# Weights of a second token stream fetched into two places of 1 MB instead of four places of 512 KB

## The reference

```
x = first_block(x, c, ctx, ...)                 # two layers, each with moe_ffn over 32 experts
return second_block(x, c_2, ctx_2, ...)

# second_block, layer 0
a_lat = x_lat * (1 + sc1) + sh1
a_ctx = x_ctx * (1 + csc1) + csh1
m_lat, m_ctx = mixer(a_lat, a_ctx, lp, rope, n_rows, not last)     # the same weights for both
x_ctx = layer_norm_2(DEEPNORM_ALPHA * x_ctx + (1 + cg1) * m_ctx, ln1_g[l], ln1_b[l])
f_ctx = swiglu(x_ctx * (1 + csc2) + csh2, w_ffn_gate[l], w_ffn_up[l], w_ffn_down[l])
```

## Time and profile before

| | |
|---|---|
| median of three runs | 3012.84 us |
| profiled execution: its time / its span | 3007.24 us / 3005.4 us |
| PE busy | 2720.4 us, 91% |
| DVE, ACT, POOL busy | 789.2, 456.2, 74.8 us |
| granted TensorE clock, mean | 0.958 |
| moved by the DMA engines | 764.86 MB, 254 GB/s over the span |
| of it the main stream's queue q1 | 680.57 MB |
| of it POOL's queue q0 | 74.26 MB |

### The profile page before, as it was taken

One profiled execution on the slowest core, in us unless ns is written; L12 is line 12 of the kernel. 1 busy time (PEld: TensorE's weight loads), 2 busy tenths in 40 slices (PEclk: granted clock), 3 DMA queues, 4 the chain that ended last, 5 costly groups with the idle time before them and its releaser, 6 DMA issues.

```text
span 3005.4 us, 33995 instructions
## 1 busy us (share of the span) xinstructions
PE 2720.4 (91%) x13754; PEld 1855.5 (62%) x13754; DVE 789.2 (26%) x1893; ACT 456.2 (15%) x973; POOL 74.8 (2%) x144
## 2 busy tenths in 40 slices
PE   6998988889989969988999779998999899998998
PEld 3554544445567754555555555687788646687887
DVE  1344202222121252111111333613642214413002
ACT  2132102121120021000000113401000123301000
POOL 0000000000000000000000000000000000000000
PEclk9998998989999979999999889999999999999999
DMA  9884898999977518999999622143675221233330
GB/s 402 332 337 186 364 414 342 372 415 411 422 305 273 224 71 330 412 418 422 416 422 422 275 83 102 70 155 114 250 278 225 113 84 56 85 142 137 141 140 15
DMA packets 117628, 764.86 MB, mean 254 GB/s; under 512 B 12832, under 2 KB 15648, under 8 KB 34272
## 3 DMA queue, kind: packets, MB, share of 16 engines
q1 hardware_dynamic: 94400, 680.57, 56.1%
q0 software_dynamic: 20224, 74.26, 6.4%
q10 hardware_dynamic: 2848, 7.83, 0.7%
HBM read 759.20 MB, written 3.41 MB: 254 GB/s over the span
## 4 chain that ended last, share of the span: by engine, by line
PE 76%; DMA 14%; DVE 6%; issue 2%; ACT 1%; SPq 1%; POOL 0%; ACTq 0%; DVEq 0%
PE bank L552 73%; DMA ring<-in_stream 13%; PE bank L851 1%; PE bank L840 1%; SPq L431 1%; DMA work<-in_stream 1%; PE bank L556 1%; DVE MX L1913 0%; DVE work L1851 0%; ACT work L1446 0%; DVE work L1930 0%; DVE work L1710 0%; DVE work L1703 0%; DVE X L2130 0%; ACT work L1376 0%
## 5 line engine op out<-in xcount | busy, mean ns | idle before, releaser
L552 PE MATMUL bank<-A,ring 128*128 128x256 f32 (+1 forms) x3088 | 712.4, 390 | 14.8 <-issue 7.7
L552 PEld LDWEIGHTS bank<-A,ring 128*128 128x128 f32 x3088 | 590.1, 192 | 131.4 <-issue 44.2
L552 PE MATMUL bank<-ring,A 128*32 128x512 f32 (+3 forms) x2304 | 413.2, 635 | 84.0 <-DMA ring<-in_stream 73.4
L552 PE MATMUL bank<-work,ring 128*128 128x256 f32 x1696 | 384.0, 383 | 5.7 <-DVE work L2382 2.1
L552 PEld LDWEIGHTS bank<-work,ring 128*128 128x128 f32 x1696 | 322.3, 191 | 57.0 <-issue 3.9
L552 PE MATMUL bank<-work 128*64 128x128 f32 (+5 forms) x2084 | 339.5, 333 | 14.8 <-DVE work L1788 5.2
L552 PEld LDWEIGHTS bank<-ring,A 128*32 128x32 f32 (+2 forms) x2304 | 129.6, 129 | 350.4 <-issue 221.0
L552 PE MATMUL bank<-A,work 128*128 128x256 f32 x1280 | 293.4, 386 | 20.0 <-ACT A L1344 11.4
L552 PEld LDWEIGHTS bank<-work 128*128 128x128 f32 (+2 forms) x2084 | 248.1, 172 | 79.1 <-issue 44.3
L552 PEld LDWEIGHTS bank<-A,work 128*128 128x128 f32 x1280 | 242.8, 193 | 79.7 <-issue 33.6
L552 PE MATMUL bank<-work,par_sb 128*128 128x256 f32 (+2 forms) x228 | 81.9, 498 | 66.2 <-DVE work L1703 15.5
(11 more groups left out here) (268 smaller groups left out, 1524.7 us busy)
## 6 DMA issues: line engine op xcount, KB each, us to landing
ring<-in_stream SPq DMA_DIRECT2D x648, 1024.0 KB, 12.7
work<-in_stream POOLq DMA_DIRECT2D x134, 512.0 KB, 8.8
X<-in_xt ACTq DMA_DIRECT2D x1, 2048.0 KB, 13.8
spill<-work ACTq DMA_DIRECT2D x3, 512.0 KB, 9.7
work<-spill POOLq DMA_DIRECT2D x3, 512.0 KB, 5.3
tab_sb<-in_tab_a ACTq DMA_DIRECT2D x1, 1120.0 KB, 18.5
X<-in_ctx2t ACTq DMA_DIRECT2D x1, 1024.0 KB, 15.9
out<-X SPq DMA_DIRECT2D x4, 256.0 KB, 2.3
```

Of the source, the lines that this page charges most:

```text
L552: return pay(pe.matmul(o, w, x, start=start, stop=stop, tile_position=place), tells)
```

## The change

```diff
-QTILES, QRING = 8, 4
+QTILES, QRING = 16, 2
```

## The result

The changed kernel takes 3034.27 us (median of 11 runs, 3023.42 to 3047.18), the kernel before 3006.83 us in 11 runs on the same chip. The ratio is 1.0079, with a 95% interval of 1.0059 to 1.0099: slower by 0.6 to 1.0%. One run of the experiments, of the kernel "rest", took 5618.34 us instead of some 3010 and is left out of its ratio.

What follows compares the result with a forecast made beforehand. PE was taken to bound the kernel, except where it waits for weights. Unhidden stall and clock loss of 18.3 us less 3.4 at the start gave 14.9, taken as +15 us: 3028 us, range 3009 to 3045 us.

Steps and rivals of the forecast that it cites:

- Landing: Context pieces beside ring traffic: a 1 MB piece lands 10.0 us after issue, against 8.8 us for 512 KB.
- The turns by rows: Context and ring queues alternate one partition row each, 4 KB against 8 KB before, so 1 MB lands 1.2 us later.
- Stalls: PE's waits for late context pieces: 5 x 4.0 + 3.6 + 3.2 + 0.8 = 27.6 us more.
- The six places with 10.0 us of room: Six context pieces with 10.0 us from possible issue to need: they come just in time, without a stall.
- The start: First context stage: the second 1 MB piece lands sooner than the old fourth piece, gaining 3.4 us.
- 7 x 1.7 = 11.9 us: Behind each of seven stalls PE's clock is halved for 3.4 us, costing 1.7 us each.
- What hides: Ring waits absorb part of the 39.5 us gross loss at the seven stalls, leaving 18.3 us.
- 5.7, against 6.5: 0: Stall at 1597 us: its 5.7 us loss hides fully in 6.5 us of ring waits, leaving 0.
- Rival 1: Expert stretches with full DMA engines: reserve suffices or stalls hide fully; +5 us, 3018 us; chance 0.22.
- Rival 2: Context transfers: larger rows are cheaper and the reserve suffices; -7 us, 3006 us; chance 0.08.
- Rival 3: Pieces land later, six more places stall, nothing hides: +50, perhaps a third hidden, +33, 3046 us; 0.20 together with rival 4.
- Rival 4: Transfers cut into 4 KB rows again, landing in 12.5 us: about +40, 3053 us; 0.20 together with rival 3.

Runs made afterwards that it cites:

- rest: Kernel before, with 57 of the 67 pieces at 1 MB, all but ten tight places, which keep two pieces of 512 KB; 3014.19 us, 1.0007.
- Split: Changed kernel's places and release, but each piece fetched as two 512 KB transfers, PE waiting for both; 3064.62 us, 1.0172 against the kernel before.
- filled: Changed kernel plus seven dummy matmuls ahead of each of the seven late pieces; 3013.38 us, 1.0006 against the kernel before.
- filler: Kernel before, 512 KB pieces, plus seven dummy matmuls at each of the seven places late at 1 MB; 3014.69 us, 1.0019.
- seven: Kernel before, with 1 MB pieces at the seven late places only; 3033.0 us, 1.0067.
- late: Changed kernel's release by 16 tiles, but two 512 KB transfers with a wait each; 3014.4 us, 1.0006 against the kernel before.
- small: Kernel before, with context pieces of 4 tiles (256 KB) in eight places; 3006.39 us, 0.9986.
- start: Kernel before, with only its first 32 context tiles as two 1 MB transfers; 3003.71 us, 0.9976, and on another chip 3006.19 us, 0.9999.
- combo: Kernel before, with first 32 context tiles as two 1 MB transfers and all later ones as 256 KB pieces; 3001.19 us, 0.9979.
- The third profile: The changed kernel unaltered, profiled a third time on the chip of the last experiments; one run, 3028.18 us.
- The two timed comparisons: The changed kernel against the kernel before, first 3034.27 us, 1.0079, then the same kernel again, 3022.45 us, 1.0050.

## Why the prediction came out as it did

**Landing: right.** 9.7 us against 10.0. The turns by rows, worked out from 3.7 us for 512 KB, carried to 1 MB. The second piece of the start came 5.7 us after the first and not 5.0, so the turns are not quite even. "Split" shows the same bytes in 4 KB rows to be later by 2.3 to 3.7 us at the same places.

**Stalls: right.** Nine waits with 28.1 us were measured, where the start's 3.2 us count in. Forecast were 27.6 us in eight places beside the start, measured 24.9. Seven were to be 3.2 to 4.0 us; six are 3.1 to 3.8, the one at 834 us is 2.6. The one at 422 us is 1.4 instead of 0.8. The six places with 10.0 us of room didn't stall, but closely: at the first of them the piece issued at 761.63 us landed 9.6 us later, and PE's first matmul on it started at 771.66, 0.5 us after the landing. "Split", 2.5 us later by its rows, has six further stalls of 1.7 to 3.1 us.

**The start: right.** -2.9 to -3.6 us against -3.4.

**The clock behind each stall: right in sum in two profiles, and by luck.** "7 x 1.7 = 11.9 us" took each stretch at 3.4 us, as after the wait of 2.89 us. In the first profile three of seven are 6.8 us: 34.0 us at half speed, up to 17 us of PE's time (15.4 when the part in which PE still stood is taken off), 4 to 5 more than forecast. In the other two the stretches sum to 23.8 us, just the 11.9 forecast, but as two of 6.8, three of 3.4 and two of none. That each stall brings 3.4 us is wrong.

**What hides: right in sum, wrong in two terms.** The seven places were to leave 18.3 us, and left 19.1, 16.5 and 16.2 us in the three profiles, when the 4.1 us of the "issue" wait are taken from the last place. At 834 us less was lost than forecast (1.8 in two profiles against 4.9): the stall was 2.3 and 2.4 us instead of 3.2, and the clock did not fall behind it. At 1597 us the step "5.7, against 6.5: 0" failed: 3.6 to 4.0 us were lost. The working had the reserve at 6.8 us and PE 5.7 us late. PE was some 7 us late (the lag grows by 6.9 us there), the DMA engines ran dry for 2.7 us, and only the first of the three ring waits went. That the hole kept the others is argued. The changed kernel, from 1618 to 1685 us of its own time, against the 6.5 us of the earlier trace rows:

```profile
PE bank L552 <- DMA ring<-in_stream: 5.6, 2, 3.4
```

**What the prediction didn't have.** At 1692 us PE restarts behind the expert stage. Before, it waited 3.5 us there for ScalarE; the row of the kernel before:

```profile
1691.99 6.10 PE L552 MATMUL bank<-work,par_sb 128*128 128x256 f32 x16 [3.52 <-ACT work L1446]
```

In the changed kernel it waits 7.6 to 7.8 us for nothing the profile shows, in all three profiles. The instruction queue q8 moves one packet of 0.02 MB in the window from 1718 to 1719 us, 2 to 3 us ahead of PE's start at 1721.03:

```profile
q8 instruction: 1, 0.02, 7.1%
```

In the kernel before such a packet comes between 1693 and 1694 us, when PE is already at work. The Trainium skill, "Runtime: NRT & Kernel Launch", section "Instruction fetch mechanics", says that an engine's instructions are fetched in blocks of 16 KiB, and that the cost of crossing a block is mostly hidden. The packet's size agrees; that PE waits for this fetch, and that it is not hidden here, is a reading and not shown. The long wait is in the three kernels that have many fewer waits on PE (changed, rest, split) and the two that have 49 more matmuls ahead of that point (filled, filler), and in none of before, seven, late, small, start and combo. So it seems to go by where a block ends in PE's program, as the short wait of small and combo at 868 us may. Filled and filler, with 21 more matmuls ahead of that place, speak for it: there the wait of 7.9 us falls into two, the second behind a few matmuls that the other kernels run without a break. Filler's timeline, where the first of them is the matmul at 868.71 of the kernel before:

```profile
874.43 0.89 PE L553 MATMUL bank<-A,work 128*128 128x256 f32 x3 [2.36 <-issue]
880.07 4.37 PE L553 MATMUL bank<-A,work 128*128 128x256 f32 x13 [4.75 <-issue]
```

Still, no run shifts the program and nothing else: it is argued from where the wait appears, not shown.

**The rivals.** Rival 1, that lateness hides nearly everywhere, comes near the truth for lateness alone (filler, 1 to 6 us for 21), and fails in the changed kernel. Rival 2 fails: the rate beside the ring did not rise, 405 and 415 GB/s. The Trainium skill, "DMA: Bandwidth & Descriptors", section "Bandwidth", favours DMAs of 1 MiB; for bandwidth that may be, but no run here shows a gain from it except the 3 us at the start, where both pieces are waited for. Rival 3's six further stalls are absent. Rival 4 is refuted by the packets and was built as "split".

**Size.** +15 us was forecast. The third profile, without the open stretch at half clock, gains 16.5 us of lag from 240 us to the end, against -3.6 (start) + 16.2 (places) + 4.1 (issue) = 16.7. The first gains 34.0 and the second 26.2 us, 21.3 and 13.5 without the 12.7 of that stretch. In the third, 3.6 us at 1597 us and the 4.1 of the "issue" wait, neither foreseen, stood against 1.2, 0.8 and 3.1 us too much at 714, 807 and 834 us. The mechanism was right; that the sum came out so near is in part luck. The two timed comparisons gave +0.79% and +0.50%, 24 and 15 us; the first may hold runs with the open stretch, which its profile shows: the four slowest of its 11 runs, 3039 to 3047 us, have a granted clock of 0.946 to 0.950, the others 0.952 to 0.956.

## What to carry to other kernels

When a buffer is cut into fewer and larger places, count the room from the release of the whole new place to the first use of it, at every piece and not in the median: seven of 67 decided here. Price a stall of an otherwise dense TensorE with what the clock may do behind it (nothing, 3.4 or 6.8 us at half speed here), and add that to the lateness before asking whether the other queue's reserve covers it. A difference of 0.1 to 0.3% can sit in an "issue" wait that the edit moved by accident, so compare those waits before crediting the edit.

## What was unexpected about the hardware

- Dummy matmuls of 21 us in seven stalls made the kernel 9 us faster than the same kernel idle there (3013.4 against 3022.5 us on one chip).
- Rows of 2 KB, 16 KB apart in memory, travelled two to a packet of 4 KB: 22,288 packets on the queue where 34,176 would be needed for rows of 2 KB.
- The "issue" wait at a restart of PE beside full DMA engines was 7.6 to 7.9 us in five kernels where six others waited 3.5 us for ScalarE, and at another restart 2.4 us in two kernels (small, combo) instead of 7.9 before, and split in two in two others (filled, filler).
- The same stall isn't always followed by the same stretch at half clock: that of 3.8 to 3.9 us at 714 us had 6.8 us behind it in one profile and 3.4 us in two, those of 2.3 to 3.1 us at 807 and 834 us had 3.4 us in one and none in two, and one of 3.4 us at 964 us (late) had none.
